# A two-block network on one core: one product copied earlier, and rows of a side computation moved between two loops

## The chip, the core and the metric

The kernel runs on one core of a Trainium2 chip. TensorE multiplies, VectorE (DVE) and ScalarE (ACT) work on whole tiles, GpSimd (POOL) mostly issues DMAs here, SyncE (SP) issues the other DMAs. The metric is the device time of one execution in microseconds, median of three runs.

## The reference

Two blocks of depth 2 over one sequence of 512 tokens of width 1024, in float32. The change lies in the first block: its four feed-forward networks, and the "adaLN" rows that modulate its sub-layers.

```python
D_MODEL, SEQ, DEPTH, N_MOD, D_FF = 1024, 512, 2, 9, 2816

def swiglu(h, w_in, w_out):
    gate, up = jnp.split(h @ w_in, 2, axis=-1)
    return (jax.nn.silu(gate) * up) @ w_out

def modulated_sublayer(x, mod, g_pre, g_post, fn, weight):
    shift, scale, gate = mod[:, 0], mod[:, 1], mod[:, 2]
    h = rmsnorm(x, g_pre) * (1.0 + scale) + shift
    y = rmsnorm(fn(h), g_post)
    return x + weight * (1.0 + gate) * y

def first_block(x, c, ada_w, ada_b, norm_g, ffn_w_in, ffn_w_out, ...):
    sc = jax.nn.silu(c)
    for i in range(DEPTH):
        mod = (sc @ ada_w[i] + ada_b[i]).reshape(B, N_MOD, D_MODEL)
        x = modulated_sublayer(x, mod[0:3], ..., swiglu(ffn_w_in[i, 0], ffn_w_out[i, 0]), 0.5)
        x = modulated_sublayer(x, mod[3:6], ..., pool_mixer if i == 0 else mla_mixer, 1.0)
        x = modulated_sublayer(x, mod[6:9], ..., swiglu(ffn_w_in[i, 1], ffn_w_out[i, 1]), 0.5)
    return x
...
def reference(...):
    return second_block(first_block(...), ...)
```

## The kernel before

Float32 products are made of three passes over split numbers: every weight tile `w` ("unit", 128 x 1024) becomes `w_hi` (ACT, `split_hi`, L464) and `w_lo = w - w_hi` (DVE, `split_lo`, L479 or L476), and TensorE computes hi·hi, lo·hi and hi·lo (`three_passes`, L506). `w_hi` and `w_lo` are rings of four units (`RING`): ACT may write unit u only when the product of unit u-4 is done.

**The four networks** `ffn0` to `ffn3` have the same plan. The first four units make two columns of the hidden layer. Then ten `pairs` follow (j = 0 to 9, seven units each, numbered r = 0 to 6 below), which compute the hidden layer by a scheme of seven half-size products with sums of weights and sums of products. Then comes `down`, 24 units in eight groups of three: the second matrix. Unit r = 3 of a pair is `split_lo(u + 3)` and so on; r = 7, 8, 9 in a pair's code are the first three units of the next pair.

**Weights of a pair.** SP loads five tiles: `a11`, `a12` into `raw`, `a21`, `a22` and `last` into the three slots of `xr`. DVE adds them in `xr[:, 1]` (`sum_1` L1266, `sum_2` L1271, `sum_4` L1275), which gives three of the units. One more unit, r = 4, is `a21 + a11`: `add_weights` on POOL (L1412) issues a DMA that adds `a11` from memory onto `xr[:, 0]`, after `sum_1` has read it. ACT's `split_hi(u + 4)` waits for this DMA to land, DVE's `split_lo(u + 4)` for ACT.

**Products of a pair** are kept by ACT out of PSUM (`keep_act`, L1156): `p1` into `std`, `p5` into `rstd`, `u2` and `u3` into `sq`. TensorE's unit r = 4 accumulates into the bank of `u2`, and so waits for that copy; unit r = 2 waits for the copy `p1`. In pair 0 the operands t_hi and t_lo of the combined input are still being made (`combine_hi_act`, `combine_lo_dve`, `combine_t4_dve`).

**The adaLN rows.** `mod` is a matrix-vector product done on DVE: one row is a 128 x 1024 multiply with an accumulated sum (`ada_block_dve`, L960), over `ada_raw`, a buffer of two tiles. POOL loads them with `ada_piece` (L1420): the load of row t waits until row t-2 is computed (`mod_blocks`). `ffn0` carries 48 rows, `ffn1` and `ffn2` 40 each, `ffn3` none. Two tables spread them: `FIRST_PAIR` gives two rows in each of the pairs 1 to 8 (16 rows), `DOWN_ROWS` the rows after unit k of `down`. All engines run their instructions in the order of the code; POOL's order in a pair is the row loads of this pair, and then `add_weights` of the next (`ffn_pool`).

**Into down.** The hidden layer `a` is split too: ACT `a_hi_act`, DVE `a_lo_dve` (L1177), eleven tiles i = 0 to 10. The unit k of `down` waits for the tiles that it multiplies: k = 0 for i = 3, k = 1 for i = 7, k = 2 for i = 10. DVE's `a_lo_dve(8 + k)` stands in the loop over k, behind `split_lo` of unit k + 2 and ahead of the rows of k.

Of the kernel before, what the change touches and what calls it, by code (L numbers as in the profile page):

```python
# [21 lines left out]
PAIRS = (NF - 2) // 2  # L22
# [99 lines left out]
def kernel_program(nc, stream, ada, xT, params, consts, constsr, pool_band, mla_rope, rope_cst,  # L122
                   pos, w2, held, out, NU):
    col = param_columns()
    with ExitStack() as ctx:
# [330 lines left out]
        def split_hi(act, u):  # L456

            if u >= own["units"]:
                return
            tile, ready, count = source[u]  # L460
            act.wait_ge(ready, count)
            if u >= RING:
                act.wait_ge(prod.sem, prod.at(("u", u - RING)))
            act.activation(w_hi[:, u % RING], tile, ACT.Copy,  # L464
                           scale=-1.0 if u in negated else 1.0).then_inc(hi_ready, 1)
# [489 lines left out]
        def ada_block_dve(dve, t):  # L955

            j, n = divmod(t, NC)
            dve.wait_ge(ada_loaded[t % 2], 16 * ((t - 2 * NC) // 2 + 1))
            row, b = ada_raw[:, t % 2], col.at["ada_b"] + NC * j
            dve.scalar_tensor_tensor(out=row, in0=row, scalar=1.0, in1=silu_row[:], op0=ALU.mult, op1=ALU.mult,  # L960
                                     accum_out=mod[:, j, n:n + 1]).then_inc(mod_blocks, 1)
            if n == NC - 1:
                dve.wait_ge(mod_blocks, NC * j)
                dve.tensor_tensor(mod[:, j], mod[:, j], par[:, b:b + NC], ALU.add).then_inc(mod_biased, 1)
# [32 lines left out]
        def follow(dve, own_order, L, y):  # L997
# [4 lines left out]
            else:  # L1002
# [2 lines left out]

        ADA = {"ffn0": range(2, 8), "ffn1": range(8, 13), "ffn2": range(13, 18), "ffn3": ()}
        SHIFT_BY_PE = (1, 2, 4, 6)
        FIRST_PAIR = {"ffn0": 1, "ffn1": 1, "ffn2": 1}
        FIRST_ROWS = {"ffn0": 0, "ffn1": 0, "ffn2": 0}
        DOWN_ROWS = {"ffn0": (0, 1, 1, 2, 2, 1, 2, 2, 1, 2, 2, 1, 2, 2, 1, 2, 2, 1, 2, 2, 1, 0, 0, 0),  # L1010
                     "ffn1": (0, 1, 1, 1, 1, 1, 1, 2, 1, 1, 2, 1, 1, 2, 1, 1, 1, 2, 1, 1, 1, 0, 0, 0)}
        DOWN_ROWS["ffn2"] = DOWN_ROWS["ffn1"]


        def ada_blocks_dve(dve, L, first, count):

            for t in range(NC * ADA[L][0] + first, NC * ADA[L][0] + first + count):
                ada_block_dve(dve, t)

        def ada_pair_dve(dve, L, j, m):  # L1020

            if ADA[L] and FIRST_PAIR[L] <= j < PAIRS - 1:
                ada_blocks_dve(dve, L, FIRST_ROWS[L] + 2 * (j - FIRST_PAIR[L]) + m, 1)

        def ada_down_dve(dve, L, k):

            if ADA[L]:
                ada_blocks_dve(dve, L, FIRST_ROWS[L] + 2 * (PAIRS - 1 - FIRST_PAIR[L]) + sum(DOWN_ROWS[L][:k]), DOWN_ROWS[L][k])

        def pair_banks(j):  # L1030

            return (0, 2, 1) if j % 2 else (7, 4, 5)
# [11 lines left out]
        def kept(name):  # L1044

            return {"p1": std[:], "p5": rstd[:], "u2": sq[:, 0], "u3": sq[:, 1]}[name]
# [103 lines left out]
        def keep_act(act, L, j, name, r, until):  # L1150

            act.wait_ge(prod.sem, prod.at(("u", own[L, j] + r)))
            if j:
                act.wait_ge(joined.sem, joined.at((L, j - 1, until)))
            b = pair_banks(j)[2 if name == "p5" else 1]
            snap.give(act.activation(kept(name), psum[:, b], ACT.Copy), (L, j, name))  # L1156

        def gate_act(act, L, j, side):

            act.wait_ge(joined.sem, joined.at((L, j, ("g1", "g2")[side])))  # L1160
            value.give(act.activation(ta[:, side], ta[:, side], ACT.Silu), (L, j, side + 1))
# [3 lines left out]
        def a_hi_act(act, L, i):  # L1165

            act.wait_ge(prod.sem, prod.at(("u", own[L, PAIRS - 1] + A_HI_AFTER[i])))
            if i:
                act.wait_ge(joined.sem, joined.at((L, i - 1, "m1")))
            else:  # L1170
                act.wait_ge(evac.sem, evac.at(("g", own[L, "g"] + 3)))
            a_hi_ready.give(act.activation(a_two_hi(i), a_two(i), ACT.Copy, scale=-1.0 if i else 1.0), (L, i))
# [8 lines left out]
        def pair_act(act, L, j):  # L1181
            u, final = own[L, j], j == PAIRS - 1
            split_hi(act, u + 3)
            keep_act(act, L, j, "p1", 0, "g1")
            split_hi(act, u + 4)
            if final:
                a_hi_act(act, L, 0)
            keep_act(act, L, j, "p5", 1, "v2")
            split_hi(act, u + 5)
            if final:  # L1190
                a_hi_act(act, L, 1)
            if j == 0:
                combine_hi_act(act, L, T4)
            keep_act(act, L, j, "u2", 2, "g2")
            split_hi(act, u + 6)
            if final:
                a_hi_act(act, L, 2)
                a_hi_act(act, L, 3)
            split_hi(act, u + 7)
            if final:  # L1200
                a_hi_act(act, L, 4)
            keep_act(act, L, j, "u3", 4, "m2")
            split_hi(act, u + 8)
            gate_act(act, L, j, 0)
            if final:
                a_hi_act(act, L, 5)
            split_hi(act, u + 9)
            gate_act(act, L, j, 1)
            if final:
                a_hi_act(act, L, 6)  # L1210
                a_hi_act(act, L, 7)
# [56 lines left out]
        def sum_2_dve(dve, L, j):  # L1268
            if j < PAIRS:
                loaded(dve, L, j, "a11")  # L1270
                summed.give(dve.tensor_tensor(xr[:, 1], xr[:, 1], home[L, j, "a11"][0].tile, ALU.add), (L, j, 2))  # L1271
# [12 lines left out]
        def up_sum_dve(dve, L, j):  # L1284

            dve.wait_ge(snap.sem, snap.at((L, j, "u3")))
            joined.give(dve.tensor_tensor(sq[:, 1], sq[:, 1], rstd[:], ALU.add), (L, j, "v2"))
# [10 lines left out]
        def pair_dve(dve, L, j):  # L1298
            u, final = own[L, j], j == PAIRS - 1
            split_lo(dve, u + 3)  # L1300
            if j:
                products_dve(dve, L, j - 1)
            split_lo(dve, u + 4)
            sum_4_dve(dve, L, j)
            if j == 0:
                combine_t4_dve(dve, L)
            if final:
                a_lo_dve(dve, L, 0)
            split_lo(dve, u + 5)
            ada_pair_dve(dve, L, j, 0)  # L1310
            if final:
                a_lo_dve(dve, L, 1)
            if j == 0:
                combine_lo_dve(dve, L, T4)
            split_lo(dve, u + 6)
            ada_pair_dve(dve, L, j, 1)
            if final:
                a_lo_dve(dve, L, 2)
            gate_sum_dve(dve, L, j, 0)
            split_lo(dve, u + 7)  # L1320
            sum_1_dve(dve, L, j + 1)
            if final:
                a_lo_dve(dve, L, 3)
            split_lo(dve, u + 8)
            sum_2_dve(dve, L, j + 1)
            up_sum_dve(dve, L, j)
            if final:
                a_lo_dve(dve, L, 4)
            gate_sum_dve(dve, L, j, 1)
            split_lo(dve, u + 9)  # L1330
            if final:
                a_lo_dve(dve, L, 5)
# [81 lines left out]
        def ada_piece(pool, t):  # L1414

            if t == 2 * NC:
                pool.wait_ge(shift_by_dve, NC - len(SHIFT_BY_PE))
            else:
                pool.wait_ge(mod_blocks, t - 1 - NC)
            pool.dma_start(ada_raw[:, t % 2], ada[t]).then_inc(ada_loaded[t % 2], 16)  # L1420

        def ffn_pool(pool, L):

            if L in ("ffn0", "ffn3"):
                add_odd(pool, L)
                add_weights(pool, L, 0)
            else:
                add_weights(pool, L, 0)
                add_odd(pool, L)
            t = ADA[L][0] * NC + (0 if L == "ffn0" else 2) if ADA[L] else 18 * NC  # L1430
            if ADA[L]:
                for _ in range(FIRST_ROWS[L] + (2 if L == "ffn0" else 0)):
                    ada_piece(pool, t)
                    t += 1
            for j in range(PAIRS):
                if ADA[L] and FIRST_PAIR[L] <= j < PAIRS - 1:
                    ada_piece(pool, t)
                    ada_piece(pool, t + 1)
                    t += 2
                add_weights(pool, L, j + 1)  # L1440
            if ADA[L]:
                for t in range(t, min((ADA[L][-1] + 1) * NC + 2, 18 * NC)):
                    ada_piece(pool, t)
# [2371 lines left out]
```

## Time and profile before

| what | value |
|---|---|
| median of 3 runs | 2932.2 us (2930.58 to 2932.82) |
| the profiled execution | 2932.32 us, its span 2930.5 us |
| busy: PE, DVE, ACT, POOL | 2805.9 us (96%), 2185.0 us (75%), 1448.7 us (49%), 401.0 us (14%) |
| mean granted TensorE clock | 0.984 |
| pairs of ffn0, ffn1, ffn2, ffn3 start at about | 56, 488, 852, 1484 us |
| down of ffn0 starts at about | 256 us |

The table is read so: the span is the time between the first and the last instruction of one profiled execution, and a change of the span shows up one to one in the run's time, which was 1.8 us longer. A busy share says how long an engine worked, not whether anybody waited for it. Times in rows below are from the start of the span.

### The profile page before, as it was taken

What the parts mean: (1) busy time and instruction counts of PE and PEld (TensorE: products, weight loads), DVE (VectorE), ACT (ScalarE), POOL (GpSimd) and SP (SyncE); (2) the same over time, 40 slices, a digit from 0 to 9 for tenths busy, and PEclk for the clock granted to TensorE, in tenths of its full rate; (3) what the DMA queues carried; (4) which work ended last, traced back from release to release, by engine and by line L of the source; (5) the groups of instructions that cost most, each with busy time, mean ns of one, the idle gap of its engine ahead of it and who ended that gap; (6) DMA issues with size and microseconds to landing.
All of it is one profiled execution on the core that took longest, in us unless ns stands there. A gap on an engine that the chain in (4) does not pass through costs nothing. (4 is left out here: it accounts for less than half of the span.)

```text
span 2930.5 us, 42964 instructions
## 1 busy us (share of the span) xinstructions
PE 2805.9 (96%) x16774; PEld 2451.4 (84%) x16774; DVE 2185.0 (75%) x3427; ACT 1448.7 (49%) x2390; POOL 401.0 (14%) x297
## 2 busy tenths in 40 slices
PE   8999989999999999799999999999899999999999
PEld 7998778998889988677799988787788778877887
DVE  7888778888778877899687755387677663866773
ACT  6555235555255542566465632464555435555552
POOL 0010111000101001100300000404300233141003
PEclk9999999999999999999999999999999999999999
DMA  7675733665636656200245432402211232022113
GB/s 271 194 224 172 238 126 76 207 203 174 233 115 214 208 168 215 73 12 19 101 119 162 145 107 87 136 15 83 91 52 58 96 127 72 30 94 72 54 56 115
DMA packets 103065, 367.40 MB, mean 125 GB/s; under 512 B 11984, under 2 KB 14800, under 8 KB 102352
## 3 DMA queue, kind: packets, MB, share of 16 engines
q1 hardware_dynamic: 73968, 262.95, 25.8%
q0 software_dynamic: 26304, 90.19, 11.7%
q10 hardware_dynamic: 2592, 11.51, 1.1%
q8 instruction: 134, 2.20, 0.3%
q14 instruction: 67, 0.55, 0.1%
HBM read 354.12 MB, written 6.29 MB: 123 GB/s over the span
## 5 line engine op out<-in xcount | busy, mean ns | idle before, releaser
L464 ACT ACTIVATE w_hi<-raw 128x1024 fp32r<-128x1024 f32 x351 | 366.8, 1053 | 320.1 <-DMA raw<-stream_in 179.1
L485 POOL TENSOR_TENSOR w_lo<-raw,w_hi 128x1024 fp32r<-128x1024 f32 x109 | 274.2, 2522 | 1265.1 <-ACT w_hi L464 1265.0
L506 PE MATMUL psum<-h_hi,w_hi 128*128 128x256 f32 (+1 forms) x1609 | 352.3, 329 | 8.5 <-DVE h_lo L699 3.4
L506 PE MATMUL psum<-h_lo,w_hi 128*128 128x256 f32 (+1 forms) x1609 | 345.4, 325 | 0.0
L506 PE MATMUL psum<-h_hi,w_lo 128*128 128x256 f32 (+1 forms) x1609 | 345.2, 325 | 0.0
L479 DVE TENSOR_TENSOR w_lo<-raw,w_hi 128x1024 fp32r<-128x1024 f32 x202 | 247.2, 1227 | 83.1 <-ACT w_hi L464 82.9
L506 PE MATMUL psum<-t_hi,w_hi 128*128 128x256 f32 (+1 forms) x1536 | 284.9, 300 | 19.9 <-ACT sq L1156 7.5
L464 ACT ACTIVATE w_hi<-xr 128x1024 fp32r<-128x1024 f32 x202 | 213.5, 1057 | 160.6 <-DVE xr L1271 68.6
L506 PEld LDWEIGHTS psum<-h_hi,w_hi 128*128 128x128 f32 x1609 | 251.0, 188 | 44.1 <-DVE w_lo L479 5.8
L506 PE MATMUL psum<-t_hi,w_lo 128*128 128x256 f32 (+1 forms) x1536 | 283.3, 299 | 0.0
L506 PEld LDWEIGHTS psum<-h_lo,w_hi 128*128 128x128 f32 x1609 | 252.0, 188 | 26.9
L506 PEld LDWEIGHTS psum<-h_hi,w_lo 128*128 128x128 f32 x1609 | 252.0, 188 | 26.3
L479 DVE TENSOR_TENSOR w_lo<-xr,w_hi 128x1024 fp32r<-128x1024 f32 x162 | 198.2, 1224 | 90.7 <-ACT w_hi L464 90.5
L506 PE MATMUL psum<-t_lo,w_hi 128*128 128x256 f32 (+1 forms) x1472 | 263.0, 295 | 0.0
L506 PEld LDWEIGHTS psum<-t_hi,w_hi 128*128 128x128 f32 x1536 | 220.9, 188 | 36.1 <-issue 9.8
L506 PEld LDWEIGHTS psum<-t_hi,w_lo 128*128 128x128 f32 x1536 | 222.5, 189 | 10.5
L506 PEld LDWEIGHTS psum<-t_lo,w_hi 128*128 128x128 f32 x1472 | 210.4, 189 | 8.0
L960 DVE SCALAR_TENSOR_TENSOR ada_raw<-ada_raw,silu_row 128x1024 f32<-128x1024 f32 x128 | 155.8, 1220 | 58.9 <-DMA ada_raw<-ada_in 58.8
L506 PE MATMUL psum<-a_lo,w_hi 128*128 128x512 f32 x704 | 176.8, 391 | 0.0
L1420 POOL DMA_DIRECT2D ada_raw<-ada_in x128 | 68.8, 541 | 717.9 <-DVE ada_raw L960 716.3
L506 PEld LDWEIGHTS psum<-a_lo,w_hi 128*128 128x128 f32 x704 | 132.2, 188 | 28.9
L1639 ACT ACTIVATE pt_hi<-psum 128x512 fp32r<-128x512 f32 (+3 forms) x160 | 74.7, 467 | 120.4 <-PE psum L1590 118.5
(527 smaller groups left out, 5568.4 us busy)
## 6 DMA issues: line engine op xcount, KB each, us to landing
raw<-stream_in SPq DMA_DIRECT2D x351, 512.0 KB, 3.4
ada_raw<-ada_in POOLq DMA_DIRECT2D x128, 512.0 KB, 5.3
xr<-stream_in SPq DMA_DIRECT2D x122, 512.0 KB, 4.6
xr<-stream_in POOLq DMA_DIRECT2D x40, 512.0 KB, 5.5
ada_in_t<-ada_in SPq DMA_DIRECT2D x8, 512.0 KB, 12.0
x_held<-X ACTq DMA_DIRECT2D x2, 2048.0 KB, 6.8
X<-x_held ACTq DMA_DIRECT2D x2, 2048.0 KB, 7.9
X<-xT_in SPq DMA_DIRECT2D x4, 512.0 KB, 5.5
```

Source lines behind the costliest of these rows:

```text
L464: act.activation(w_hi[:, u % RING], tile, ACT.Copy, scale=-1.0 if u in negated else 1.0).then_inc(hi_ready, 1)
L479: op = dve.tensor_tensor(w_lo[:, u % RING], source[u][0], low, ALU.subtract)
L485: pool.tensor_tensor(w_lo[:, u % RING], source[u][0], w_hi[:, u % RING].bitcast(F32), ALU.subtract).then_inc(lo_ready, 1)
L506: mm = pe.matmul(dst, w[wi], m[mi], start=(first and n == 0), stop=(last and n == total - 1), skip_group_check=skip)
L960: dve.scalar_tensor_tensor(out=row, in0=row, scalar=1.0, in1=silu_row[:], op0=ALU.mult, op1=ALU.mult, accum_out=mod[:, j, n:n + 1]).then_i ...
L1420: pool.dma_start(ada_raw[:, t % 2], ada[t]).then_inc(ada_loaded[t % 2], 16)
L1639: turned_hi.give(act.activation(A["place"](0, t, rows, n, i), psum[0:rows, 6 + k % 2, 0:n * P].rearrange("p (a n) -> p a n", n=P), ACT.Cop ...
```

## The change

In all four networks ACT's copy `u2` of pair 0 moves ahead of `split_hi(u + 5)` and of `combine_hi_act(T4)`. In the other pairs its place stays.

The rows of `ffn0` are spread otherwise: pairs 1 and 2 carry two rows, pairs 3 to 8 three, which makes 22; `down` carries 26 and not 32. The third row of a pair stands on DVE behind `sum_2` and ahead of `up_sum`. `ffn1` and `ffn2` keep 16 rows in pairs and 24 in down. In all three networks the first row of `down` is now computed at k = 2 and not at k = 1, and the rows with two in one unit are spread evenly. POOL issues the loads of a pair by the same table, still ahead of `add_weights`.

```diff
-        FIRST_PAIR = {"ffn0": 1, "ffn1": 1, "ffn2": 1}
+        PAIR_ROWS = {"ffn0": (0, 2, 2, 3, 3, 3, 3, 3, 3, 0), "ffn1": (0,) + 8 * (2,) + (0,),
+                     "ffn2": (0,) + 8 * (2,) + (0,)}
...
-        DOWN_ROWS = {"ffn0": (0, 1, 1, 2, 2, 1, 2, 2, 1, 2, 2, 1, 2, 2, 1, 2, 2, 1, 2, 2, 1, 0, 0, 0),
-                     "ffn1": (0, 1, 1, 1, 1, 1, 1, 2, 1, 1, 2, 1, 1, 2, 1, 1, 1, 2, 1, 1, 1, 0, 0, 0)}
+        DOWN_ROWS = {"ffn0": (0, 0, 1, 2, 1, 1, 2, 1, 1, 2, 1, 1, 2, 1, 1, 2, 1, 1, 2, 2, 1, 0, 0, 0),
+                     "ffn1": (0, 0, 1, 1, 2, 1, 1, 2, 1, 1, 2, 1, 1, 2, 1, 1, 2, 1, 1, 1, 1, 0, 0, 0)}
...
         def ada_pair_dve(dve, L, j, m):
-            if ADA[L] and FIRST_PAIR[L] <= j < PAIRS - 1:
-                ada_blocks_dve(dve, L, FIRST_ROWS[L] + 2 * (j - FIRST_PAIR[L]) + m, 1)
+            if ADA[L] and m < PAIR_ROWS[L][j]:
+                ada_blocks_dve(dve, L, FIRST_ROWS[L] + sum(PAIR_ROWS[L][:j]) + m, 1)
...
@@ pair_act
             keep_act(act, L, j, "p5", 1, "v2")
+            if j == 0:
+                keep_act(act, L, j, "u2", 2, "g2")
             split_hi(act, u + 5)
...
             if j == 0:
                 combine_hi_act(act, L, T4)
-            keep_act(act, L, j, "u2", 2, "g2")
+            else:
+                keep_act(act, L, j, "u2", 2, "g2")
             split_hi(act, u + 6)
...
@@ pair_dve
             sum_2_dve(dve, L, j + 1)
+            ada_pair_dve(dve, L, j, 2)
             up_sum_dve(dve, L, j)
...
@@ ffn_pool
             for j in range(PAIRS):
-                if ADA[L] and FIRST_PAIR[L] <= j < PAIRS - 1:
+                for _ in range(PAIR_ROWS[L][j] if ADA[L] else 0):
                     ada_piece(pool, t)
-                    ada_piece(pool, t + 1)
-                    t += 2
+                    t += 1
                 add_weights(pool, L, j + 1)
```

ACT in pair 0 of `ffn0`, before: `std` and `rstd` are the copies p1 and p5, the first `sq` is u2, `t_hi` is the combined input.

```order
L1156 ACTIVATE std<-psum 128x512
L464 ACTIVATE w_hi<-xr 128x1024
L1156 ACTIVATE rstd<-psum 128x512
L464 ACTIVATE w_hi<-xr 128x1024
L1219 ACTIVATE t_hi<-t_sum 128x1024
L1156 ACTIVATE sq<-psum 128x512
```

And in the changed kernel:

```order
L1157 ACTIVATE std<-psum 128x512
L464 ACTIVATE w_hi<-xr 128x1024
L1157 ACTIVATE rstd<-psum 128x512
L1157 ACTIVATE sq<-psum 128x512
L464 ACTIVATE w_hi<-xr 128x1024
L1223 ACTIVATE t_hi<-t_sum 128x1024
```

The copy into `sq` moved ahead of one weight split and one split of the input.

POOL in `ffn0` before, from the `add_weights` of pair 3 (the first row) to that of pair 5 (the last), with the semaphores that each waits for:

```order
L1412 DMA xr<-stream_in 128x1024 [waits weights_summed,pair_loaded0]
L1420 DMA ada_raw<-ada_in 128x1024 [waits mod_blocks] x2
L1412 DMA xr<-stream_in 128x1024 [waits weights_summed,pair_loaded0]
L1420 DMA ada_raw<-ada_in 128x1024 [waits mod_blocks] x2
L1412 DMA xr<-stream_in 128x1024 [waits weights_summed,pair_loaded0]
```

And the same stretch in the changed kernel:

```order
L1417 DMA xr<-stream_in 128x1024 [waits weights_summed,pair_loaded0]
L1425 DMA ada_raw<-ada_in 128x1024 [waits mod_blocks] x3
L1417 DMA xr<-stream_in 128x1024 [waits weights_summed,pair_loaded0]
L1425 DMA ada_raw<-ada_in 128x1024 [waits mod_blocks] x3
L1417 DMA xr<-stream_in 128x1024 [waits weights_summed,pair_loaded0]
```

A third row load, with its wait, stands ahead of each `add_weights` from pair 4 to pair 9.

DVE in pair 3 of `ffn0`, before, from the second row to the last split of that pair's code (`xr<-xr` is `sum_1`, the next `xr<-xr,raw` `sum_2`, `sq<-sq,rstd` `up_sum`):

```order
L960 SCALAR_TENSOR_TENSOR ada_raw,mod<-ada_raw,silu_row 128x1024
L1282 TENSOR_TENSOR ta<-std,psum 128x512
L479 TENSOR_TENSOR w_lo<-raw,w_hi 128x1024
L1266 TENSOR_TENSOR xr<-xr 128x1024
L479 TENSOR_TENSOR w_lo<-xr,w_hi 128x1024
L1271 TENSOR_TENSOR xr<-xr,raw 128x1024
L1287 TENSOR_TENSOR sq<-sq,rstd 128x512
L1282 TENSOR_TENSOR ta<-sq,psum 128x512
```

And in the changed kernel:

```order
L960 SCALAR_TENSOR_TENSOR ada_raw,mod<-ada_raw,silu_row 128x1024
L1286 TENSOR_TENSOR ta<-std,psum 128x512
L479 TENSOR_TENSOR w_lo<-raw,w_hi 128x1024
L1270 TENSOR_TENSOR xr<-xr 128x1024
L479 TENSOR_TENSOR w_lo<-xr,w_hi 128x1024
L1275 TENSOR_TENSOR xr<-xr,raw 128x1024
L960 SCALAR_TENSOR_TENSOR ada_raw,mod<-ada_raw,silu_row 128x1024
L1291 TENSOR_TENSOR sq<-sq,rstd 128x512
L1286 TENSOR_TENSOR ta<-sq,psum 128x512
```

The third row stands behind `sum_2`, two weight tiles later than `sum_1`, whose end is what `add_weights` waited for.

## Rows read from the trace of the kernel before

**Rows 1.** The page: busy time of TensorE, share of the span, instructions.

```profile
PE 2805.9 (96%) x16774; PEld 2451.4 (84%) x16774; DVE 2185.0 (75%) x3427; ACT 1448.7 (49%) x2390; POOL 401.0 (14%) x297
```

**Rows 2.** Timeline, PE: start, us, line, tiles, and idle time before with releaser.

```profile
69.73 0.74 PE L506 MATMUL psum<-t_hi,w_hi 128*128 128x256 f32 x4 [1.88 <-ACT sq L1156]
...
262.89 0.70 PE L506 MATMUL psum<-t_hi,w_hi 128*128 128x512 f32 x2 [0.82 <-DVE a_lo L1177]
270.12 0.71 PE L506 MATMUL psum<-t_hi,w_hi 128*128 128x512 f32 x2 [1.49 <-DVE a_lo L1177]
...
342.20 0.73 PE L506 MATMUL psum<-t_hi,w_hi 128*128 128x512 f32 x2 [1.79 <-DVE w_lo L479]
364.83 0.74 PE L506 MATMUL psum<-t_hi,w_hi 128*128 128x512 f32 x2 [1.59 <-DVE w_lo L479]
376.99 0.74 PE L506 MATMUL psum<-t_hi,w_hi 128*128 128x512 f32 x2 [2.25 <-DVE w_lo L479]
...
695.79 0.70 PE L506 MATMUL psum<-t_hi,w_hi 128*128 128x512 f32 x2 [0.19 <-DVE a_lo L1177]
...
1059.16 0.70 PE L506 MATMUL psum<-t_hi,w_hi 128*128 128x512 f32 x2 [0.81 <-DVE a_lo L1177]
```

**Rows 3.** Timeline, ACT, pair 0 of ffn0: copy p5, split of unit 5, copy u2.

```profile
62.25 0.59 ACT L1156 ACTIVATE rstd<-psum 128x512 f32<-128x512 f32 x1
67.00 1.06 ACT L464 ACTIVATE w_hi<-xr 128x1024 fp32r<-128x1024 f32 x1 [4.16 <-DVE xr L1275]
...
69.10 0.58 ACT L1156 ACTIVATE sq<-psum 128x512 f32<-128x512 f32 x1
```

**Rows 4.** Timeline, DVE, ffn0: pair 3 into pair 4, then pair 9.

```profile
122.80 1.22 DVE L479 TENSOR_TENSOR w_lo<-xr,w_hi 128x1024 fp32r<-128x1024 f32 x1
...
126.28 1.23 DVE L479 TENSOR_TENSOR w_lo<-xr,w_hi 128x1024 fp32r<-128x1024 f32 x1 [1.13 <-ACT w_hi L464]
127.42 1.22 DVE L960 SCALAR_TENSOR_TENSOR ada_raw<-ada_raw,silu_row 128x1024 f32<-128x1024 f32 x1
...
132.58 1.22 DVE L1266 TENSOR_TENSOR xr<-xr 128x1024 f32<-128x1024 f32 x1
...
137.20 0.69 DVE L1287 TENSOR_TENSOR sq<-sq,rstd 128x512 f32<-128x512 f32 x1
...
142.82 1.23 DVE L479 TENSOR_TENSOR w_lo<-xr,w_hi 128x1024 fp32r<-128x1024 f32 x1 [0.26 <-ACT w_hi L464]
...
242.36 1.22 DVE L479 TENSOR_TENSOR w_lo<-xr,w_hi 128x1024 fp32r<-128x1024 f32 x1
...
261.53 1.22 DVE L1177 SCALAR_TENSOR_TENSOR a_lo<-a,t_lo 128x1024 fp32r<-128x1024 f32 x1
```

**Rows 5.** Timeline, POOL, pair 3 of ffn0: its first row load, `add_weights` of pair 4.

```profile
128.94 0.55 POOL L1420 DMA_DIRECT2D ada_raw<-ada_in  x1 [13.39 <-DVE ada_raw L960]
...
134.35 0.88 POOL L1412 DMA_DIRECT2D xr<-stream_in  x1 [2.60 <-DVE xr L1266]
```

**Rows 6.** One line's instructions, L1412: the issue at 134.35; 60 to 240 us.

```profile
DMA to landing us min/median/max: 7.4/7.4/7.4
...
DMA to landing us min/median/max: 5.3/6.3/7.4
```

**Rows 7.** The same for L1420: two issues just behind an `add_weights`; the whole run.

```profile
L1420 POOL DMA_DIRECT2D ada_raw<-ada_in x2: 899/900/900, 54.4 to 54.9; - x2
...
DMA to landing us min/median/max: 6.9/7.2/7.6
...
DMA to landing us min/median/max: 3.4/5.3/8.0
```

**Rows 8.** Timeline, DVE: pair 1 of ffn1, pair 1 of ffn2, pair 2 of ffn3.

```profile
516.47 1.23 DVE L479 TENSOR_TENSOR w_lo<-xr,w_hi 128x1024 fp32r<-128x1024 f32 x1 [0.81 <-ACT w_hi L464]
...
870.15 1.23 DVE L1266 TENSOR_TENSOR xr<-xr 128x1024 f32<-128x1024 f32 x1 [0.25 <-DMA xr<-stream_in]
...
1532.85 1.23 DVE L479 TENSOR_TENSOR w_lo<-xr,w_hi 128x1024 fp32r<-128x1024 f32 x1 [0.61 <-ACT w_hi L464]
```

More of the change, by code:

```diff
@@ L1020, in ada_pair_dve @@
         def ada_pair_dve(dve, L, j, m):
-            if ADA[L] and FIRST_PAIR[L] <= j < PAIRS - 1:
-                ada_blocks_dve(dve, L, FIRST_ROWS[L] + 2 * (j - FIRST_PAIR[L]) + m, 1)
+            if ADA[L] and m < PAIR_ROWS[L][j]:
+                ada_blocks_dve(dve, L, FIRST_ROWS[L] + sum(PAIR_ROWS[L][:j]) + m, 1)
         def ada_down_dve(dve, L, k):
             if ADA[L]:
-                ada_blocks_dve(dve, L, FIRST_ROWS[L] + 2 * (PAIRS - 1 - FIRST_PAIR[L]) + sum(DOWN_ROWS[L][:k]), DOWN_ROWS[L][k])
+                ada_blocks_dve(dve, L, FIRST_ROWS[L] + sum(PAIR_ROWS[L]) + sum(DOWN_ROWS[L][:k]), DOWN_ROWS[L][k])
         def pair_banks(j):
```

## The prediction, made before the changed kernel was timed

> **What bounds the kernel now.** I read the page first: TensorE is busy for 96% of the span [rows 1], so time is won or lost only where it waits. So the second view is TensorE's own timeline, its rows with idle time ahead of them [rows 2]. In the four networks these are: in pair 0 a wait of 1.88 us for ACT's copy `u2` (69.73; the same in all four); at the second unit of `down` (k = 1) a wait for `a_lo`, 0.82, 0.19 and 0.81 us in ffn0, ffn1 and ffn2; at k = 2 another of 1.49 us (270.12; the same in these three); and in the down of ffn0 three waits for `w_lo`, 1.79, 1.59 and 2.25 us, together 5.63. The third view is DVE's timeline over the pairs [rows 4]: `split_lo(u + 4)` of pairs 3 and 9 of ffn0 start at 122.80 and 242.36, six pairs in 119.56 us, 19.9 each, and the idle times between are waits for ACT. TensorE has no idle row in that stretch, yet the wait at 262.89 ends with an `a_lo` that started at 261.53: by the end of the pairs DVE's chain sets the time, not TensorE. The fourth view is POOL's [rows 5] and the landings of its DMAs [rows 6, 7].
>
> **The earlier copy.** Copy p5 ended at 62.84 and `split_hi(u + 5)` then waited 4.16 us for `sum_4`; the copy behind it started at 69.10 [rows 3]. TensorE's unit 2, whose product is copied, was done long before. In its new place the copy runs inside that wait, and TensorE wins the whole 1.88 us in pair 0. Nothing is behind it that it delays: the split that followed waits until 67.00 anyway. But DVE's chain isn't moved: `split_lo(u + 5)` still hangs on `sum_4`, and only the next split comes some 0.28 us sooner (0.58 copy less the waiting). So what is kept depends on who is late at k = 1:
> - ffn3 has no rows. There DVE waits for splits that stand behind copies of TensorE's products (0.61 us in one pair of many alike) [rows 8]: DVE follows TensorE, and the 1.88 us are kept.
> - ffn1: one such wait, 0.81 us in pair 1 [rows 8]. DVE can come forward by this; the wait of 0.19 us at k = 1 grows by the rest. I take 0.81 us, between 0.8 and 1.9.
> - ffn2: the same place has no such wait, and `sum_1` waits for an SP load (0.25 us) [rows 8] that is issued by a step that doesn't move. DVE's chain is where it was, 0.81 us late at k = 1 [rows 2]: kept 0, at most 0.3.
> - ffn0: 0.28, counted in DVE's chain below.
>
> **The first row of down a unit on.** One row is 1.14 us of DVE from start to start (126.28 to 127.42 [rows 4] is that pitch for a tile of this size). It stood ahead of `a_lo(10)`, for which k = 2 waits. Without it the wait of 1.49 us becomes 0.35: -1.14 us in each of ffn0, ffn1, ffn2. The row itself then lies in a unit where DVE has room (no `w_lo` wait in the downs of ffn1 and ffn2). Even spreading there: nothing, at most 0.5 either way.
>
> **Six rows fewer in the down of ffn0.** It had five rows per three units, and each pair of rows is bound by the double buffer: row t's load is issued when t-2 is done. With four rows per three units the backlog that made TensorE wait three times goes: -5.63 us, bounded by -4.
>
> **Six rows more in the pairs of ffn0: the term that decides.** On DVE alone a third row adds 1.14 us to a chain of about 19.7 us. But POOL is in order. In pairs 3 to 8 it must now issue a third row load ahead of `add_weights` of the next pair, and this load waits for the third row of the same pair, which DVE computes behind `sum_2`. Before, `add_weights` had only `sum_1` to wait for. Who waits behind it: ACT's `split_hi(u + 4)` for its landing, DVE's `split_lo(u + 4)` for ACT, and everything of DVE behind that. From one `split_lo(u + 4)` to the next, by rows:
> - to the place of the third row: 137.20 - 122.80 = 14.40 [rows 4] (it takes the place of `up_sum`);
> - from a row's start to its load's issue on POOL: 128.94 - 127.42 = 1.52 [rows 4, 5];
> - the issue of that load ahead of `add_weights`: 0.55 [rows 5];
> - landing of `add_weights`: 5.3 to 7.4, median 6.3, in these pairs [rows 6], where 3 us separate it from the load ahead of it. Now 0.55 separates them. The nearest row is two loads just behind an `add_weights`, 6.9 and 7.6 [rows 7]. I take 6.9; ends 5.3 and 7.6;
> - from landing to `split_lo`: issued at 134.35, landed 7.4 later at 141.75, `split_lo` at 142.82: 1.07 [rows 4, 5, 6].
>
> The sum is 14.40 + 1.52 + 0.55 + 6.9 + 1.07 = 24.44 us per pair (22.84 to 25.14). The last of these rows is also proof that the landing is on DVE's path: with 7.4 us DVE already waited 0.26. The delay reaches pairs 4 to 9, six times: 6 x 24.44 = 146.6 against 119.56, +27.1; less the 0.28 of the copy, plus 0.17 for an addition of the bias that falls in another place: **+27.0 us** (17.4 to 31.2). DVE leads TensorE by some 5 us there: TensorE's unit 4 started at 69.73 in pair 0 [rows 2], so three periods of 19.9 later, in pair 3, at 129.4, and its `split_lo` ended at 124.0 [rows 4]. So TensorE starts to wait in pair 4 or 5 and then waits in every pair. None of it is absorbed by the end, since k = 1 waited for this very chain already (0.82). Does TensorE hold DVE in its turn? Its unit 4 now waits for copy `u2`, behind ACT's delayed splits, some 5 us after the landing; three units of 2.84 us (19.9 over seven) later it is at 13.5 us, and DVE reads these products 16 us and more after the landing. So no.
>
> **Sum, against the profiled execution (2932.32 us, 0.1 above the median).** ffn0: +27.0 - 1.14 - 5.63 = +20.2. ffn1: -0.81 - 1.14 = -1.95. ffn2: -1.14. ffn3: -1.88. Together +15.3: 2947.6, or **2947.5 us** beside the median of 2932.2. Ends: with 5.3 us landing 2937.9, with 7.6 us 2951.7; the other terms can take 1.5 off and put 2 on.
>
> **Rival 1: the landing is short and DVE's own chain decides (faster).** If `add_weights` landed within 20.90 - 17.54 = 3.4 us of its issue (20.90 is DVE's chain without the landing, 142.82 - 0.26 - 122.80 = 19.76 [rows 4], and 1.14; 17.54 the other four terms), a third row would cost only its own 1.14 us: 6 x 20.90 = 125.4 against 119.56, with the copy and the bias +5.7. Sum: 5.7 - 6.8 - 5.0 = -6.1: 2926.1 us. Against it: the shortest of all row loads of the run took 3.4 us, the shortest of nine `add_weights` here 5.3 [rows 6, 7]. Chance 0.07.
> The Trainium skill gives this rival as a rule: "DMA: Bandwidth & Descriptors", section "Anatomy of one DMA — SWDGE (gpsimd) path", puts a DMA issued from GpSimd at 2.0 us plus the bytes at 436 per ns, by which 512 KB would take an estimated 3.2 us and the time would be 2926.1. This trace disagrees with its 5.3 to 7.4 us.
>
> **Rival 2: the lead swallows a part.** If TensorE's wait at k = 1 were set by something that a lead of 3 to 4 us (5 less the 1.88 won ahead of it) covers, the loss would be smaller by it: 2944. The wait of 0.82 us for `a_lo` at 262.89 speaks against it. Chance 0.07.
>
> **Rival 3: down of ffn0 keeps its waits.** The last three units with rows still carry 2, 2 and 1, as before, and two of the three waits stood there. If these come from these units alone and not from a backlog, 3.8 us stay: 2951.4. For it: the place. Against it: DVE may split unit 20 when unit 16 is done, five units of down before unit 22, each about 5 us (376.99 - 364.83 less 2.25 for two [rows 2]): 25 us. The five rows in there take two each 1.52 + 5.3 us [rows 5, 7], 17 in all. Chance 0.06.
>
> **How the numbers follow.** Forecast as summed 0.80, rivals 0.07, 0.07, 0.06. Its low end, with short landings, lies at 2936, so a little of it falls within 0.2% (5.9 us, about what a measurement of this kernel can tell from no change). Slower 0.85, same 0.07, faster 0.08. Range 2936 to 2954: the forecast with both ends of the landing, and rivals 2 and 3.
>
> **What would show it.** Right: POOL's `add_weights` of pairs 4 to 9 of ffn0 issued some 6.7 us after `sum_1` starts and not 1.8; six DVE periods of 23 to 25 us; ACT's `split_hi(u + 4)` waiting for that DMA for some 3 us; TensorE idle in pairs 5 to 9, most at unit 4; no wait of 1.88 us in any pair 0; 0.35 at k = 2; no `w_lo` waits in the down of ffn0; k = 1 waits of about 1.3 us in ffn1 and 2.7 in ffn2. Wrong: DVE periods near 20.8 (rival 1), or `add_weights` issued as early as before, in which case I misread POOL's order.

## The result, and the profile after

| | before | changed |
|---|---|---|
| median, runs | 2931.39 us (2929.68 to 2932.82, 4 runs) | 2946.43 us (2943.59 to 2950.11, 4 runs) |
| ratio, 95% interval | | 1.0052 (1.0035 to 1.0069) |
| the profiled execution, its span | 2932.32, 2930.5 us | 2943.59, 2941.8 us |

The change makes the kernel slower, by 15 us between the medians; 15.3 were forecast. The profiled execution is the shortest of the four, so its trace shows 11.3 us. The interval of the ratio leaves room for 10 to 20 us.

TensorE's line of the page (answers to [rows 1]), and ACT in pair 0 of ffn0 (answers to [rows 3]):

```profile
PE 2807.6 (95%) x16774; PEld 2453.2 (83%) x16774; DVE 2185.0 (74%) x3427; ACT 1438.0 (49%) x2390; POOL 400.1 (14%) x297
...
65.11 0.60 ACT L1157 ACTIVATE sq<-psum 128x512 f32<-128x512 f32 x1 [1.75 <-PE psum L506]
67.52 1.06 ACT L464 ACTIVATE w_hi<-xr 128x1024 fp32r<-128x1024 f32 x1 [1.81 <-DVE xr L1279]
```

TensorE has the same work in a longer span. The copy now ends at 65.71, 4 us before it did, and the split of unit 5 still starts when `sum_4` is done.

Timeline of POOL in the changed kernel, pair 3 of ffn0 up to the `add_weights` of pair 4 (answers to [rows 5]; L1425 is a row load, L1417 `add_weights`), and the landings of L1417 from 140 to 270 us (answers to [rows 6]):

```profile
130.55 0.54 POOL L1425 DMA_DIRECT2D ada_raw<-ada_in  x1 [13.39 <-DVE ada_raw L960]
...
140.34 0.53 POOL L1425 DMA_DIRECT2D ada_raw<-ada_in  x1 [6.97 <-DVE ada_raw L960]
140.85 0.91 POOL L1417 DMA_DIRECT2D xr<-stream_in  x1
...
L1417 POOL DMA_DIRECT2D xr<-stream_in x6: 909/910/915, 140.9 to 267.0; - x6
...
  ACT w_hi L464: 30.1, 6
...
DMA to landing us min/median/max: 7.3/7.5/7.8
```

POOL waited 6.97 us for DVE's third row with `add_weights` behind it. `sum_1` had started at 134.19, so `add_weights` came 6.66 us after it, where it had come 1.77 after [rows 4, 5]. It took 7.3 to 7.8 us to land, and ACT waited for it 30.1 us in six pairs, 5.0 each, where some 3 had been forecast.

Timeline of DVE in the changed kernel (answers to [rows 4]): `split_lo(u + 4)` of pairs 3, 4, 5 and 9, and the third rows between.

```profile
124.41 1.22 DVE L479 TENSOR_TENSOR w_lo<-xr,w_hi 128x1024 fp32r<-128x1024 f32 x1
...
138.81 1.22 DVE L960 SCALAR_TENSOR_TENSOR ada_raw<-ada_raw,silu_row 128x1024 f32<-128x1024 f32 x1
...
149.31 1.23 DVE L479 TENSOR_TENSOR w_lo<-xr,w_hi 128x1024 fp32r<-128x1024 f32 x1 [3.99 <-ACT w_hi L464]
...
163.91 1.22 DVE L960 SCALAR_TENSOR_TENSOR ada_raw<-ada_raw,silu_row 128x1024 f32<-128x1024 f32 x1
...
174.68 1.23 DVE L479 TENSOR_TENSOR w_lo<-xr,w_hi 128x1024 fp32r<-128x1024 f32 x1 [4.26 <-ACT w_hi L464]
...
275.43 1.23 DVE L479 TENSOR_TENSOR w_lo<-xr,w_hi 128x1024 fp32r<-128x1024 f32 x1 [4.01 <-ACT w_hi L464]
```

Six periods took 275.43 - 124.41 = 151.0 us, 25.2 each, against 119.56 before.

Timeline of TensorE (answers to [rows 2]): waits from pair 4 on, the units k = 1 and k = 2 in the down of ffn0, the first wait behind that down, and the waits at k = 1 in ffn1 and ffn2:

```profile
153.29 1.22 PE L506 MATMUL psum<-t_hi,w_hi 128*128 128x256 f32 x4 [3.98 <-ACT sq L1157]
178.66 1.08 PE L506 MATMUL psum<-t_hi,w_hi 128*128 128x256 f32 x4 [3.68 <-ACT sq L1157]
...
280.36 1.22 PE L506 MATMUL psum<-t_hi,w_hi 128*128 128x256 f32 x4 [4.70 <-ACT sq L1157]
296.44 0.71 PE L506 MATMUL psum<-t_hi,w_hi 128*128 128x512 f32 x2
...
302.53 0.70 PE L506 MATMUL psum<-t_hi,w_hi 128*128 128x512 f32 x2 [0.34 <-DVE a_lo L1178]
...
418.70 1.16 PE L591 MATMUL psum<-ident,stat 128*128 128x128 f32 x8 [0.26 <-DVE stat L841]
...
716.36 0.71 PE L506 MATMUL psum<-t_hi,w_hi 128*128 128x512 f32 x2 [1.34 <-DVE a_lo L1178]
...
1077.25 0.71 PE L506 MATMUL psum<-t_hi,w_hi 128*128 128x512 f32 x2 [1.34 <-DVE a_lo L1178]
```

TensorE now waits in every pair from 4 to 9, at unit 4, for the copy `u2`. The three waits for `w_lo` in the down of ffn0 are gone, k = 1 has no wait (296.44), k = 2 waits 0.34 us, and no pair 0 has a wait for `u2`. In ffn2 k = 1 waits 1.34 us, where about 2.7 had been forecast; 1.3 in ffn1 is as forecast.

### The profile page after: what moved, and what is told of

Same layout as the page of the kernel before. It is cut to its first block and busy times, and to the rows that moved or that the text cites. A ratio compares the mean times of both kernels' runs of the same rounds, so it can differ in the third digit from the quotient of the medians.

```text
span 2941.8 us, 42964 instructions
## 1 busy us (share of the span) xinstructions
PE 2807.6 (95%) x16774; PEld 2453.2 (83%) x16774; DVE 2185.0 (74%) x3427; ACT 1438.0 (49%) x2390; POOL 400.1 (14%) x297
## 5 line engine op out<-in xcount | busy, mean ns | idle before, releaser
L1425 POOL DMA_DIRECT2D ada_raw<-ada_in x128 | 68.5, 538 | 748.2 <-DVE ada_raw L960 745.7
```

## The experiments

Each is an edit of the changed kernel, except one of the kernel before. The ratios are to the kernel before as it was timed beside each experiment: its median was 2931.63 us in the first four and 2933.41 us in the last two. The question was first whether POOL's order is the cause, and then what the rest of the change is worth.

### POOL's order

```diff
@@ ffn_pool
-                for _ in range(PAIR_ROWS[L][j] if ADA[L] else 0):
+                rows = PAIR_ROWS[L][j] if ADA[L] else 0
+                for _ in range(min(rows, 2)):
                     ada_piece(pool, t)
                     t += 1
                 add_weights(pool, L, j + 1)
+                for _ in range(rows - 2):
+                    ada_piece(pool, t)
+                    t += 1
```

> The changed kernel, but POOL issues add_weights ahead of the third row load of each pair and not behind it; DVE and all tables as changed. Theory (POOL holds add_weights back for the third row): the six DVE periods of pairs 4 to 9 of ffn0 fall from 25.2 us to 20.9 (19.76 and one row of 1.14), 125.4 us in place of 151.0, and the time from 2946 to about 2921 us, which is below the kernel before. Rival (the third row costs by itself, on DVE or by its DMA beside the others): the periods stay above 24 us and the time within 4 us of 2946.

Measured: 2922.24 us (2920.39 to 2924.96), 0.9968 of the kernel before (0.9955 to 0.9981). POOL and DVE of this run, pair 3 and then `split_lo(u + 4)` of pairs 3 and 9, and the landings of its `add_weights`:

```profile
135.21 0.87 POOL L1417 DMA_DIRECT2D xr<-stream_in  x1 [2.60 <-DVE xr L1270]
139.59 0.55 POOL L1425 DMA_DIRECT2D ada_raw<-ada_in  x1 [3.51 <-DVE ada_raw L960]
...
123.66 1.22 DVE L479 TENSOR_TENSOR w_lo<-xr,w_hi 128x1024 fp32r<-128x1024 f32 x1
...
249.59 1.22 DVE L479 TENSOR_TENSOR w_lo<-xr,w_hi 128x1024 fp32r<-128x1024 f32 x1
...
DMA to landing us min/median/max: 5.3/5.6/6.0
```

Six periods take 125.9 us (125.4 expected): DVE's own chain with one row more, and nothing else. Same DVE order, same number of rows, same DMAs: one DMA issue moved past one other, once in each of six pairs, is worth 24 us. The rival falls. The landing was also shorter, 5.3 to 6.0 us and not 7.3 to 7.8; in this run nothing waits for it any more.

### Two rows in the pairs again

```diff
-        PAIR_ROWS = {"ffn0": (0, 2, 2, 3, 3, 3, 3, 3, 3, 0), ...
+        PAIR_ROWS = {"ffn0": (0,) + 8 * (2,) + (0,), ...
-        DOWN_ROWS = {"ffn0": (0, 0, 1, 2, 1, 1, 2, 1, 1, 2, 1, 1, 2, 1, 1, 2, 1, 1, 2, 2, 1, 0, 0, 0),
+        DOWN_ROWS = {"ffn0": (0, 0, 2, 2, 2, 1, 2, 2, 1, 2, 2, 1, 2, 2, 1, 2, 2, 1, 2, 2, 1, 0, 0, 0),
```

> The changed kernel with two rows in pairs 1 to 8 of ffn0 and 32 in its down (first at k = 2), so only the earlier copy and the later first row are left of the change. Theory: DVE's six periods are back at 119.6 us in all, the waits for w_lo in the down of ffn0 are back (4 to 6 us), the time is 1.9 (ffn3) + 0.8 (ffn1) + 3.4 (three times 1.14) = 6 us below before: about 2925. Rival (the loss of 15 us has another part, the earlier copy, which moves TensorE against the DMAs): the time stays above 2935.

Measured: 2922.06 us (2919.59 to 2924.87), 0.9964 (0.9951 to 0.9977). Periods of pairs 4 to 9, between these two rows: 119.2 us; and one of three waits for `w_lo` in the down of ffn0, 1.94, 1.70 and 1.14 us:

```profile
122.91 1.22 DVE L479 TENSOR_TENSOR w_lo<-xr,w_hi 128x1024 fp32r<-128x1024 f32 x1
...
242.11 1.22 DVE L479 TENSOR_TENSOR w_lo<-xr,w_hi 128x1024 fp32r<-128x1024 f32 x1
...
340.95 0.73 PE L506 MATMUL psum<-t_hi,w_hi 128*128 128x512 f32 x2 [1.94 <-DVE w_lo L479]
```

So the whole loss lies in the rows of ffn0, and the other two parts are worth 9 to 10 us, where 6 were expected. And moving six rows into the pairs is worth nothing even with POOL's order mended (2922.2 against 2922.1): what the down gives, 4.8 us of waits, the pairs take back, six rows of 1.14 us on a chain for which TensorE waits at the end.

### The earlier copy alone

On the kernel before:

```diff
             keep_act(act, L, j, "p5", 1, "v2")
+            if j == 0:
+                keep_act(act, L, j, "u2", 2, "g2")
             split_hi(act, u + 5)
...
                 combine_hi_act(act, L, T4)
-            keep_act(act, L, j, "u2", 2, "g2")
+            else:
+                keep_act(act, L, j, "u2", 2, "g2")
```

> The kernel before with the earlier copy u2 in pair 0 alone. Theory (DVE's chain keeps most of it): the wait of 1.88 us is gone in all four networks, but comes back at k = 1 of down: some 2.5 us in ffn0, 1.3 in ffn1, 2.7 in ffn2, where 0.8, 0.2 and 0.8 were; only ffn3 keeps 1.9 and ffn1 0.8: 2928.7 us, 0.1% below before. Rival (TensorE's gain is kept everywhere): 4 x 1.88 = 7.5 us, 2923.9.

Measured: 2928.18 us (2924.23 to 2934.26), 0.999 (0.9979 to 1.0001): as expected in size, though the interval touches no change. What the trace shows of the mechanism, TensorE in ffn0 and ffn2:

```profile
247.71 0.50 PE L506 MATMUL psum<-t_hi,w_hi 128*128 128x256 f32 x2 [0.85 <-ACT sq L1156]
...
263.31 0.71 PE L506 MATMUL psum<-t_hi,w_hi 128*128 128x512 f32 x2 [1.36 <-DVE a_lo L1177]
270.54 0.71 PE L506 MATMUL psum<-t_hi,w_hi 128*128 128x512 f32 x2 [1.48 <-DVE a_lo L1177]
...
1039.29 0.74 PE L506 MATMUL psum<-t_hi,w_hi 128*128 128x256 f32 x4 [0.83 <-ACT sq L1156]
1054.88 0.70 PE L506 MATMUL psum<-t_hi,w_hi 128*128 128x512 f32 x2 [1.34 <-DVE a_lo L1177]
```

The wait comes back, as the theory said, but at two places: 0.83 to 0.85 us at unit 4 of pair 9, whose copy `u2` ACT makes behind DVE's late `sum_4`, and 1.34 to 1.36 at k = 1. Together 2.2 us in ffn0 and ffn2 where 0.8 stood; 2.5 and 2.7 had been expected, all of it at k = 1. In ffn1 it is 2.1 us (0.72 and 1.35) where 0.2 stood and 1.3 was expected. From the first unit of a network to its k = 2 the copy won 0.8 us in ffn1 (235.4 to 234.6), 0.5 in ffn2 (234.5 to 234.0) and 3.3 in ffn3 (234.0 to 230.8), where 0.8, 0 and 1.9 were expected. The rival, 1.9 kept in each, falls in ffn1 and ffn2. The 0.8 of ffn1 is right in size, but not as it was meant: TensorE's waits there at pairs 0 and 9, k = 1 and k = 2 add up to 3.6 us in the kernel before and in this one, so the gain lies in the stretch where its clock had been lower (the last section). In ffn0 nothing was won; this execution had a wait of 1.05 us for an SP load at `sum_1` of pair 0; in the others it is between nothing and 1.25 us. What more ffn3 gave is told in the section on the hardware.

### One pair with a third row

```diff
-        PAIR_ROWS = {"ffn0": (0, 2, 2, 3, 3, 3, 3, 3, 3, 0), ...
+        PAIR_ROWS = {"ffn0": (0, 2, 2, 2, 2, 3, 2, 2, 2, 0), ...
-        DOWN_ROWS = {"ffn0": (0, 0, 1, 2, 1, 1, 2, 1, 1, 2, 1, 1, 2, 1, 1, 2, 1, 1, 2, 2, 1, 0, 0, 0),
+        DOWN_ROWS = {"ffn0": (0, 0, 1, 2, 2, 1, 2, 2, 1, 2, 2, 1, 2, 2, 1, 2, 2, 1, 2, 2, 1, 0, 0, 0),
```

> As e2_two_rows, but one pair of ffn0 (j = 5) with a third row, and 31 rows in down; POOL's order as changed. Theory (a held add_weights delays DVE's chain, and the end of the pairs waits for this chain): one DVE period of 25.2 us among five of 19.8, TensorE waits 1 to 2 us in pair 6, the rest of the 5.4 us comes at k = 1 of down; in all 5 us above e2_two_rows less 1 for the row that down has less. Rival (DVE's lead swallows a single delay): TensorE loses less than 2 us against e2_two_rows.

Measured: 2930.16 us (2926.72 to 2933.56), 0.9995 (0.9985 to 1.0004). DVE's `split_lo(u + 4)` of pairs 5 and 6 and TensorE's waits in pair 6:

```profile
164.51 1.22 DVE L479 TENSOR_TENSOR w_lo<-xr,w_hi 128x1024 fp32r<-128x1024 f32 x1
...
189.55 1.22 DVE L479 TENSOR_TENSOR w_lo<-xr,w_hi 128x1024 fp32r<-128x1024 f32 x1 [3.69 <-ACT w_hi L464]
...
183.94 0.74 PE L506 MATMUL psum<-t_hi,w_hi 128*128 128x256 f32 x4 [1.05 <-ACT std L1157]
...
193.54 0.80 PE L506 MATMUL psum<-t_hi,w_hi 128*128 128x256 f32 x2 [3.67 <-ACT sq L1157]
```

One period of 25.04 us, as expected. But TensorE waited 4.7 us in pair 6 (behind that its granted clock was 0.50 of full speed from 194 to 198 us) and had no wait at k = 1, where 1 to 2 and the rest were expected: I had measured DVE's lead at `split_lo`, but TensorE waits for the copy `u2`, 2.8 us after that split ends (190.77 to 193.54). The total is what counts: 8 us above two rows everywhere (2930.2 against 2922.1; I expected 4). The lead swallows nothing. What goes beyond the 5.3 us of that period isn't explained by the pairs; the down of this run had 5.3 us of waits for `w_lo` against 4.8 and a granted clock of 0.97 from 300 to 400 us against 1.00, and the two medians are uncertain by some 3 us each. The two profiled executions can't settle it: they differ by 2.5 us only (2927.40 and 2924.87), 9.2 us at the end of ffn0's down and 6.7 us less behind it, where both have the same code.

### The third row ahead of `sum_1`

```diff
@@ pair_dve
             split_lo(dve, u + 7)
+            ada_pair_dve(dve, L, j, 2)
             sum_1_dve(dve, L, j + 1)
...
             sum_2_dve(dve, L, j + 1)
-            ada_pair_dve(dve, L, j, 2)
```

> The changed kernel with the third row of a pair on DVE ahead of sum_1 and not behind sum_2; POOL's order as changed. Theory (what costs is that add_weights waits for something that DVE does later than sum_1): POOL issues add_weights again 1.8 us after sum_1 starts. But the row now stands where its load has hardly landed: issued 1.5 us after the first row starts, 6.3 us to landing, needed 5.2 us after the first row starts, so DVE waits some 2.6 us for it: periods of 20.9 + 2.6 = 23.5 us, 141 in all, 10 us less than the changed kernel: about 2936 us. Rival (the number of rows alone decides, wherever they stand): periods of 25 us and 2946; or, if the load isn't late, 20.9 and 2922.

Measured: 2935.82 us (2926.87 to 2939.36), 1.0005 (0.9991 to 1.0019). The third row of pair 3, POOL behind it, and `split_lo(u + 4)` of pairs 3 and 9:

```profile
136.51 1.23 DVE L960 SCALAR_TENSOR_TENSOR ada_raw<-ada_raw,silu_row 128x1024 f32<-128x1024 f32 x1 [2.69 <-DMA ada_raw<-ada_in]
...
137.66 1.22 DVE L1270 TENSOR_TENSOR xr<-xr 128x1024 f32<-128x1024 f32 x1
...
139.43 0.87 POOL L1417 DMA_DIRECT2D xr<-stream_in  x1 [0.86 <-DVE xr L1270]
...
123.95 1.22 DVE L479 TENSOR_TENSOR w_lo<-xr,w_hi 128x1024 fp32r<-128x1024 f32 x1
...
265.27 1.22 DVE L479 TENSOR_TENSOR w_lo<-xr,w_hi 128x1024 fp32r<-128x1024 f32 x1
```

`add_weights` follows `sum_1` by 1.77 us again, the row waits 2.69 us for its load, and the six periods take 141.3 us: 141 were expected, and 2936 us. With the same number of rows there are now three times for the six periods, 125.9, 141.3 and 151.0, each by what stands in whose way. The rival falls.

### Fewer rows in the pairs, spread

The POOL order of the first experiment, and

```diff
-        PAIR_ROWS = {"ffn0": (0, 2, 2, 3, 3, 3, 3, 3, 3, 0), ...
+        PAIR_ROWS = {"ffn0": (0, 2, 3, 2, 3, 2, 3, 2, 3, 0), ...
-        DOWN_ROWS = {"ffn0": (0, 0, 1, 2, 1, 1, 2, 1, 1, 2, 1, 1, 2, 1, 1, 2, 1, 1, 2, 2, 1, 0, 0, 0),
+        DOWN_ROWS = {"ffn0": (0, 0, 1, 2, 1, 1, 2, 2, 1, 2, 1, 1, 2, 1, 1, 2, 2, 1, 2, 2, 1, 0, 0, 0),
```

> As e1_pool_order (add_weights ahead of the third row load), with 20 rows in the pairs of ffn0 (three in pairs 2, 4, 6, 8, two in the others) and 28 in down, four to five per three units. Theory (a row in the pairs costs its 1.14 us of DVE's chain, a row in down nothing until the double buffer is full): two rows fewer in the pairs give 2.3 us against e1, the down stays free of waits for w_lo or has one of under 1 us: 2920 to 2921 us. Rival (the waits for w_lo in down come from its last units with 2, 2 and 1 rows): they are back with 2 to 4 us, and the time is 2922 to 2924.

Measured: 2921.46 us (2917.57 to 2930.61), 0.9957 (0.9942 to 0.9971). One wait for `w_lo` is left in the down:

```profile
374.65 0.73 PE L506 MATMUL psum<-t_hi,w_hi 128*128 128x512 f32 x2 [0.82 <-DVE w_lo L479]
```

That is the wait of under 1 us that the theory allowed, and no rival's 2 to 4. The time is the lowest of all, 10 to 12 us under the kernel before, but can't be told from that of the first two experiments.

## Why the prediction was right

**The deciding term** was right in its mechanism and low in size. Six periods were to be 24.44 us each and were 25.2. Of the 0.7 us too little, 0.6 is the landing, 7.5 us in the middle where I took 6.9: the nearest row had row loads behind an `add_weights`, not the reverse, and its other value, 7.6, was the nearer one [rows 7]. The place of the third row (138.81 - 124.41 = 14.40), its way to POOL (1.53) and the step from landing to `split_lo` (1.1 us at 149.31) held. The Trainium skill ("DMA: Bandwidth & Descriptors", section "Anatomy of one DMA — SWDGE (gpsimd) path") gives by its fit an estimated 3.2 us; the six landings took 7.3 to 7.8 us, and the shortest of all row loads 3.4.

**The path to k = 1.** `split_lo(u + 4)` of pair 9 stands 33.1 us later than before, where 27.0 was forecast: 31.5 from the periods, and 1.6 from the start. The 1.6 are mostly a first stage 0.5 us longer and a wait of 1.25 us for an SP load in pair 0, where I had expected DVE 0.28 us earlier. By k = 2 it was 32.4 us (270.12 to 302.53): 1.14 less for the row, and 0.5 more for a wait of DVE at 286.99 that it did not have before. By the end of the down it was 24.2 (the first wait for `stat` behind it moved from 394.48 to 418.70): the down gave back 5.6 us of named waits, 1.0 of a wait for ACT's last square (389.94), and 1.5 that no listed wait names, 8.2 in all where I counted 5.63. So ffn0 is +24.2 and not +20.2. That TensorE has to wait for `u2` and not for `split_lo` I had seen, but not that this leaves no wait at k = 1. Behind the wait of 4.70 us in pair 9 (280.36) its granted clock was 0.50 until 284 us, and up to k = 1 it needed 16.1 us (280.36 to 296.44), where the first experiment, at full clock, needed 14.2 and then waited 1.7. The lower clock stands in the place of that wait, and cost at most the 0.5 us at 286.99.

**The other networks** gave more than forecast. From the first unit to k = 2: ffn1 -2.5 (forecast -1.95), ffn2 -1.65 (-1.14), ffn3 -3.7 (-1.88), together 2.9 more than forecast. The first row of down a unit on won its 1.14 us in each of three: 1.49 became 0.34, 0.25 and 0.34. The term mis-sized is the copy in ffn3, by a factor of two, and the last section says from what. A further 2.3 us came in the norm between ffn0 and ffn1, where nothing is changed: the granted clock was 0.81 from 448 to 466 us before and 1.00 from 472 to 488 us now. This stretch took 33.8 us before and in two experiments, 31.3 in the changed kernel and two others, the kernel before with the copy alone among them: it differs between executions of the same code there. Another 2.7 us net came in pieces of 1.3 or less in other stretches that the change doesn't touch. So ffn0 cost 4 us more than forecast and all behind it 8 less, 5 of them no work of the change: +11.3 us in the profiled execution and not +15.3. The medians are at +15.0; which of these pieces differ in the other executions, whose times spread over 6.5 us, no trace shows. The mechanism is borne out, but that the medians agree with the forecast to 0.3 us is luck: the errors of single terms were up to 4 us and went both ways, and the measured change is uncertain by 5 us.

**The rivals.** Rival 1 (DVE's own chain, 2926 us) is what the first experiment made: its periods of 20.9 us are there, and the time was 2922. It needed POOL's order, not a short landing. Rival 2 (the lead swallows a part) fell in the run with one pair. Rival 3 (the last units keep the waits of down) fell: with 26 rows none was left, with 28 one of 0.82 us.

## What to carry to other kernels

An engine that only issues DMAs still holds them in order: ask of each wait that is put into its queue what stands behind it and who needs that, here one issue moved past another, in six pairs, for 24 us. A row moved from a crowded loop to one whose busy share is lower is no gain if the second loop's chain ends on the path as well: both loops charged about 1 us per row. And a short wait of TensorE can cost twice its length, since the clock may fall behind it.

## What the runs showed of the hardware

**A wait of 1.9 us and the clock.** In the kernel before TensorE waited 1.88 us in pair 0 of each network. Behind two of these waits, in ffn1 and ffn3, its granted clock fell to the lower level, 1.2 GHz, for some 4 us; behind the other two it did not. TensorE in ffn3, four matmuls a row, start to start 0.47 us at 2.4 GHz:

```profile
1498.34 0.74 PE L506 MATMUL psum<-t_hi,w_hi 128*128 128x256 f32 x4 [1.88 <-ACT sq L1156]
...
1500.49 1.05 PE L506 MATMUL psum<-t_hi,w_hi 128*128 128x256 f32 x4
1501.34 1.05 PE L506 MATMUL psum<-t_hi,w_lo 128*128 128x256 f32 x4
...
1503.74 0.63 PE L506 MATMUL psum<-h_lo,w_hi 128*128 128x256 f32 x4
1504.21 0.63 PE L506 MATMUL psum<-h_hi,w_hi 128*128 128x256 f32 x4
```

From 1500.49 to 1501.34 four matmuls took 0.85 us. In the stretch 1490 to 1510 us the granted clock was 0.91 of full speed before, and 1.00 in the changed kernel's pair 0 and in all six experiments. That is the 1.4 to 1.8 us that ffn3 gave beyond the wait. In ffn1 it was 0.83 from 498 to 508 us, which is 1.7 us at full speed; DVE's chain decides there at the end of the pairs, and 0.8 us of it came back in the experiment with the copy alone. That the wait brought the clock down is inferred: seven traces without it kept 1.00 in both places, and only one trace has it. The same reading, by stretch (core 0: us, PE busy, granted clock, DMA share, GB/s), the kernel before and then the changed one in its pairs and at the start of pair 9's unit 4:

```profile
68.00:72.00 4.00, 2.27 (x19) 1.00 1.00 336
...
1500.00:1504.00 4.00, 4.00 (x27) 0.69 0.56 213
...
498.00:508.00 10.00, 8.11 (x56) 0.83 0.64 210
1490.00:1510.00 20.00, 17.90 (x135) 0.91 0.51 161
...
140.00:280.00 140.00, 117.73 (x914) 0.91 0.62 183
280.00:282.00 2.00, 1.64 (x7) 0.50 0.26 104
```

The first row is pair 0 of ffn0, where the same wait left the clock alone. The last two rows: behind the longer waits of the changed kernel the clock was lower in its pairs too. The periods show no price for that, since DVE's chain set their time (25.2 us each, of which the landing and the order of POOL account for all but 0.1).

**Two DMAs of 512 KB from POOL within 0.5 us.** `add_weights` landed 7.3 to 7.8 us after its issue with a row load issued 0.52 us ahead, in all six pairs. In the first experiment, with the load ahead of it some 3.1 us away, it took 5.3 to 6.0 us; but with the same 3.1 us it took 5.4 to 7.4 in the kernel before and 5.5 to 7.3 (median 6.9) with two rows again. With 1.4 us (the third row ahead of `sum_1`) it took:

```profile
DMA to landing us min/median/max: 5.3/5.8/6.3
```

So 0.5 us goes with the longest landings, 0.6 to 1.9 us above the medians of the others; that the nearness alone does it is not shown, since landings differ by up to 2 us at the same distance.
